# Moving the compressed branch's outputs into the local branch's PSUM banks in a hybrid attention layer

## The reference, cut to what matters

```
proj = rmsnorm(x) @ w_in
# attention: 8 heads of 128 in 2 key/value groups g, 4 heads r in each
s     = q @ kcmp * scale                         # compressed branch: 127 blocks
p_cmp = softmax(where(valid, s, NEG))
o_cmp = p_cmp @ vcmp
imp   = (p_cmp summed over the 4 heads) @ overlap # importance of 32 blocks
sel   = top 16 of imp (first and local blocks forced)
o_sel = softmax(q @ ks over selected blocks) @ vs # selected branch
o_win = softmax(q @ kw over 512 tokens) @ vw      # local branch
o     = g0 * o_cmp + g1 * o_sel + g2 * o_win
# pooling mixer: trailing means over 2/4/8/16 tokens minus the token, then a 256x256 matmul per group
h = x + concat(y_pool, o) @ w_out
h = h + (silu(n(h) @ w_gate) * (n(h) @ w_up)) @ w_down
h = h + (p @ w_ple_proj) * sigmoid(n(h) @ w_ple_gate);  out = rmsnorm(h)
```

## Time and profile before

| | |
|---|---|
| runs | 1813.19, 1814.67, 1815.13 us; median 1814.67 |
| profiled execution, its own time | 1814.66 us |
| its span on the slowest core (core 1) | 1813.1 us |
| spans of the 8 cores | 1808.7 to 1813.1 us |
| PE busy | 1678.0 us, 93% of the span |
| DVE, ACT, POOL busy | 578.7, 405.9, 279.6 us |
| attention stage, 320 to 616 us: PE busy | 241.90 of 296 us |

### The profile page before, as it was taken

The page is one execution under the profiler, slowest core; times in us unless marked ns, Lnnn a source line. Parts: engine busy times, 40 slices in busy tenths (PEclk is TensorE's granted clock), DMA queues, the critical chain, the costliest instruction groups (busy, mean ns, idle before and its releaser), DMA issues.

```text
span 1813.1 us, 25150 instructions; the slowest of 8 cores (1808.7 to 1813.1 us)
## 1 busy us (share of the span) xinstructions
PE 1678.0 (93%) x8998; PEld 825.4 (46%) x8998; DVE 578.7 (32%) x1386; ACT 405.9 (22%) x675; POOL 279.6 (15%) x339
## 2 busy tenths in 40 slices
PE   4799999788878999999999999999999999999994
PEld 1344544455545544444444444444444444444453
DVE  2663343554445313401122101311012200135556
ACT  3452212444436512100000000000000000133332
POOL 3232000012232133100000000000000000054321
PEclk9799999999989999999999999999999999999997
DMA  9565402011106920654039340583402934334413
GB/s 200 168 162 96 65 15 47 1 25 25 47 1 100 191 95 1 117 93 93 1 59 174 60 80 1 102 152 73 93 1 48 175 60 90 57 66 81 77 52 136
DMA packets 31323, 144.01 MB, mean 79 GB/s; under 512 B 4576, under 2 KB 9184, under 8 KB 22240
## 3 DMA queue, kind: packets, MB, share of 16 engines
q0 software_dynamic: 16416, 108.04, 34.0%
q1 hardware_dynamic: 14784, 34.35, 5.7%
HBM read 242.03 MB, written 8.39 MB: 138 GB/s over the span
## 4 chain that ended last, share of the span: by engine, by line
PE 84%; DVE 7%; DMA 3%; issue 3%; ACT 2%; DVEq 0%; POOL 0%; SPq 0%; ACTq 0%; POOLq 0%
PE ps L1215 17%; PE ps L1192 16%; PE ps L1189 16%; PE ps L511 11%; PE ps L1168 6%; PE ps L1293 5%; PE ps L869 3%; PE ps L738 2%; PE ps L754 2%; DMA arena<-c_sin 1%; DVE arena L1141 1%; DMA arena<-xin 1%; DVE arena L717 1%; PE ps L535 1%; DMA arena<-wup 1%
## 5 line engine op out<-in xcount | busy, mean ns | idle before, releaser
L1189 PE MATMUL ps<-arena 128*128 128x512 bf16 x1408 | 319.7, 379 | 2.0 <-DVE arena L1141 2.0
L1192 PE MATMUL ps<-arena 128*128 128x512 bf16 x1408 | 319.7, 380 | 0.8 <-DMA arena<-wup 0.8
L1215 PE MATMUL ps<-arena 128*128 128x512 bf16 x1408 | 304.9, 379 | 0.0
L1197 DVE TENSOR_TENSOR arena<-ps,arena 128x512 bf16<-128x512 f32 x88 | 60.9, 692 | 540.4 <-PE ps L1192 278.1
L1196 ACT ACTIVATE arena<-ps 128x512 f32<-128x512 f32 x88 | 52.6, 598 | 782.8 <-PE ps L1189 755.7
L1189 PEld LDWEIGHTS ps<-arena 128*128 128x128 bf16 x1408 | 137.8, 98 | 169.6 <-issue 4.9
L1192 PEld LDWEIGHTS ps<-arena 128*128 128x128 bf16 x1408 | 138.1, 98 | 168.1 <-issue 3.4
L1215 PEld LDWEIGHTS ps<-arena 128*128 128x128 bf16 x1408 | 137.8, 98 | 166.2 <-issue 0.6
L511 PE MATMUL ps<-arena 128*128 128x512 bf16 x896 | 208.2, 389 | 0.1
L1095 DVE TENSOR_TENSOR arena<-ps,arena 128x512 f32<-128x512 f32 x160 | 110.6, 691 | 275.2 <-PE ps L1215 202.4
L1107 POOL TENSOR_TENSOR arena<-arena 128x512 f32<-128x512 f32 (+2 forms) x98 | 115.4, 1178 | 232.0 <-ACT arena L1106 220.2
(11 more groups left out here) (146 smaller groups left out, 1145.1 us busy)
## 6 DMA issues: line engine op xcount, KB each, us to landing
arena<-wdown POOLq DMA_DIRECT2D x16, 1536.0 KB, 13.7
arena<-wgate POOLq DMA_DIRECT2D x22, 1024.0 KB, 9.5
arena<-wup POOLq DMA_DIRECT2D x22, 1024.0 KB, 11.0
arena<-xin SPq DMA_DIRECT2D x32, 512.0 KB, 5.5
arena<-wB POOLq DMA_DIRECT2D x20, 512.0 KB, 14.4
arena<-xT SPq DMA_DIRECT2D x16, 512.0 KB, 18.6
arena<-wout POOLq DMA_DIRECT2D x4, 2048.0 KB, 35.4
arena<-wpg POOLq DMA_DIRECT2D x4, 2048.0 KB, 23.4
```

The source lines that it names most:

```text
L1189: PE(lambda e, dc=dc: e.matmul(ps[pg][:], lhsT=wgu[sl][:, dc, half * 128:(half + 1) * 128], rhs=a2T[t][:, dc, :], start=(dc == 0), stop=(d ...
L1192: PE(lambda e, dc=dc: e.matmul(ps[pu][:], lhsT=wgu[sl + 1][:, dc, half * 128:(half + 1) * 128], rhs=a2T[t][:, dc, :], start=(dc == 0), sto ...
L1215: PE(lambda e, ci=ci: e.matmul(ps[pb][:], lhsT=wt_[:, ci, mm * 128:(mm + 1) * 128], rhs=hT[:, ci, t * 512:(t + 1) * 512], start=(ci == 0), ...
```

## The change

Three things change. (1) s1 writes the compressed outputs into banks 4 and 5, two heads in each, the banks of the local branch; only segment 0's, which is computed earlier, keeps banks 6 and 7. (2) s1 no longer closes a half-done unit, and the hold is gone: pieces come by credit alone. (3) s3 stands at step ntot-3 instead of ntot-5, ntot being the steps of the segment. The order of the heads in DVE's reads changes with the banks.

```diff
-    fstate = {"open": False, "hold": 0, "credit": 0.0}
+    fstate = {"open": False, "credit": 0.0}
...
         def bankof(r):
-            return (TB, 340) if r == 3 else (FB, 161 * r)
+            if sbank is not None:
+                return (TB, 340) if r == 3 else (FB, 161 * r)
+            return (4 + r // 2, 161 * (r % 2))
+        lead = (0, 3) if sbank is not None else (0, 2)
 
         def s1():
-            close_fill()
-            fstate["hold"] = 4
             for r in range(4):
                 bank, c0 = bankof(r)
...
-            r_, Br = branch_scale([(3, 4, ps[TB][:, 468:469]), (0, 3, ps[FB][:, 128:451:161])], [PB[TB], PB[FB]], 0, g, ot)
+            if sbank is not None:
+                den, Bden = [(3, 4, ps[TB][:, 468:469]), (0, 3, ps[FB][:, 128:451:161])], [PB[TB], PB[FB]]
+            else:
+                den, Bden = [(2, 4, ps[5][:, 128:290:161]), (0, 2, ps[4][:, 128:290:161])], [PB[5], PB[4]]
+            r_, Br = branch_scale(den, Bden, 0, g, ot)
...
-            if fstate["hold"] > 0:
-                fstate["hold"] -= 1
-            elif fill and fstate["credit"] >= 1.0 and len(fill) > 1:
+            if fill and fstate["credit"] >= 1.0 and len(fill) > 1:
                 pop_fill()
...
-                at.setdefault((0, min(4, ntot - 1), min(4, ntot - 1), 6, ntot - 5)[k], []).append(f)
+                at.setdefault((0, min(4, ntot - 1), min(4, ntot - 1), 6, ntot - 3)[k], []).append(f)
```

More of the change, by code:

```diff
@@ L786, in bankof @@
         def bankof(r):
-            return (TB, 340) if r == 3 else (FB, 161 * r)
+            if sbank is not None:
+                return (TB, 340) if r == 3 else (FB, 161 * r)
+            return (4 + r // 2, 161 * (r % 2))
+        lead = (0, 3) if sbank is not None else (0, 2)
         def s1():
-            close_fill()
-            fstate["hold"] = 4
             for r in range(4):
                 bank, c0 = bankof(r)
-                PE(lambda e, r=r, bank=bank, c0=c0: e.matmul(ps[bank][:, c0:c0 + 161], lhsT=pt[:, r, :], rhs=vcmp1[:, g, 0:161], start=(r in (0, 3)), stop=True, skip_group_check=True),
+                PE(lambda e, r=r, bank=bank, c0=c0: e.matmul(ps[bank][:, c0:c0 + 161], lhsT=pt[:, r, :], rhs=vcmp1[:, g, 0:161], start=(r in lead), stop=True, skip_group_check=True),
                    [Bpt, B_vcmp[g]], [PB[bank]])
-            r_, Br = branch_scale([(3, 4, ps[TB][:, 468:469]), (0, 3, ps[FB][:, 128:451:161])], [PB[TB], PB[FB]], 0, g, ot)
+            if sbank is not None:
[3 more added lines that the diff above has]
+            r_, Br = branch_scale(den, Bden, 0, g, ot)
             hold["r"] = (r_, Br)
@@ L799, in s1 @@
                 ib, Bi = impb[ii], B_imp[ii]
-                for n, r in enumerate((3, 0, 1, 2)):
+                for n, r in enumerate((2, 3, 0, 1)):
                     bank, c0 = bankof(r)
@@ L810, in s1b @@
             oa, B_oa = oaccs[oi % 3], B_oaccs[oi % 3]
-            for r in (3, 0, 1, 2):
+            for r in (2, 3, 0, 1):
                 bank, c0 = bankof(r)
```

## The result

The changed kernel takes 1794.7 us (median of 12 runs) against 1814.7 of the kernel before (12 runs, beside them): 20.0 us less, at a ratio of 0.9881 (95% interval 0.9841 to 0.9921). That is faster by 1.1%, and 9 us faster than the forecast of 1803.8; the range ended at 1795.

The account below looks back on a forecast made before the run. The prediction took about 54 us of idle PE in 320 to 616 us, nearly all ended by DVE's queue order, as the bound. Terms 11.7 - 7.9 - 3.9 - 6.4 - 2.4 - 2.0 = -10.9 gave 1803.8 us, range 1795 to 1813.

Parts of the forecast that it names:

- the clock: PE's granted clock in the attention stage: change put at zero, with 4 us to either side.
- term 6: Scores (L738) in steps paced by ACT, which the hold put in rows of four: idle time -2.0 us.
- term 1: s1's new wait for DVE's read of the local branch in banks 4 and 5: +11.7 us, bounds +6 and +17.
- term 2: PE's wait before the selection's transposes (L824), nearly all of it to go: -7.9 us.
- term 3: Output transposes (L724), whose bank 7 is no longer read by L813: wait gone, -3.9 us.
- term 4: Pieces (L869, L913) waiting for DVE, as compressed reads no longer hold bank 6: 12.1 to 5.7, -6.4 us.
- term 5: Pieces waiting for ACT's L917, as they now come every second step: 3.2 to 0.8, -2.4 us.
- A: Rival: without the hold, L877 queues behind compressed reads and DVE's backlog cancels the gain; +0.8, 1815.5 us; chance 0.22.
- B: Rival: new or longer waits in segments 8 to 14 bring clock dips of their own; +7, 1822 us; chance 0.07.
- C: Rival: full gain, segments 8 and 9 absorb waits, no piece waits for DVE, steps unpaced; -22, 1793 us; chance 0.12.
- D: Rival: gain doesn't reach the end, the output projection waiting for its weights or x; 1814 us; chance 0.03.

Follow-up runs that it names:

- e3: The kernel before without the hold, nothing else changed: 1843.2 us, ratio 1.0157 to the kernel before.
- e5: The changed kernel with the hold and the closing of a unit put back: 1798.7 us, ratio 0.9875 to the kernel before.
- e11: The kernel before with 16 unread matmuls in front of the selection's transposes of segments 3 and 11: 1812.5 us, ratio 0.9982.
- e8: The changed kernel with 16 and 10 unread matmuls in front of s1 in segments 8 and 9: 1793.4 us.
- e2: The kernel before with s3 two steps later and nothing else: 1804.8 us, ratio 0.994.
- e1: The kernel before with the new banks alone; hold, closing of a unit and s3's step stay: 1811.0 us, ratio 0.9992.
- e6: The changed kernel with s1 and s2 one step later in segments with ot of 2 or more: 1794.0 us.
- e7: The changed kernel with s1 and s2 two steps later in segments with ot of 2 or more: 1793.4 us.

## Why the prediction was right and wrong, by its own steps

The direction held, and so did nearly every wait; the gain was almost twice the forecast. Two steps failed: the clock was put at zero, and the hold's cost (term 6) was sized at 2.0 and looked for in listed waits. Means over the 8 cores, us:

| step | before | changed | measured | forecast |
|---|---|---|---|---|
| term 1, s1 | 18.5 | 28.4 | +9.8 | +11.7 |
| term 2, selection's transposes | 8.5 | 1.2 | -7.3 | -7.9 |
| term 3, output transposes | 3.9 | 0 | -3.9 | -3.9 |
| term 4, pieces behind DVE | 11.9 | 5.1 | -6.8 | -6.4 |
| term 5, pieces behind ACT | 3.2 | 0.9 | -2.3 | -2.4 |
| term 6, scores by ACT | 4.0 | 4.1 | +0.1 | -2.0 |
| small groups | 2.6 | 1.0 | -1.6 | 0 |
| idle in all | 52.6 | 40.7 | -11.9 | -10.9 |
| clock, PE busy | 13.2 | 10.1 | -3.1 | 0 |
| rest (waits not listed) | 230.5 | 225.8 | -4.7 | 0 |

**Term 1** was right in place, and within 2 us in size. The new waits stand where they were put; they come in pairs, as the two banks come free one after the other (segments 13 and 8, PE timeline of the changed kernel):

```profile
546.68 0.30 PE L795 MATMUL ps<-arena 128*128 128x161 bf16 x2 [1.49 <-DVE arena L717]
547.59 0.30 PE L795 MATMUL ps<-arena 128*128 128x161 bf16 x2 [0.61 <-DVE arena L717]
```

```profile
472.01 0.30 PE L795 MATMUL ps<-arena 128*128 128x161 bf16 x2 [4.10 <-DVE arena L717]
472.93 0.43 PE L795 MATMUL ps<-arena 128*128 128x161 bf16 x2 [0.61 <-DVE arena L717]
473.15 0.63 PE L738 MATMUL ps<-arena 128*128 128x512 bf16 x1
```

In segment 13 that is 1.49 + 0.61 = 2.1 us (forecast 2.4), in segment 8 4.10 + 0.61 = 4.7 (3.7), and in segment 9 2.5 (2.9).

**Terms 2 to 5** were right to 0.6 us each, by walking through the new order of PE and DVE with durations from the trace. (On core 1, from which the prediction read them, term 2 is -7.8.)

**Term 6** is one of the two steps that failed: a real effect, under-sized and looked for in the wrong place. The -2.0 was to come out of L738's listed waits, and these stayed (4.0, now 4.1). The hold's cost stands in waits that are not listed: with the hold the rest is 4.6 us higher in one pair of kernels (before and e3) and 5.7 in the other (e5 and changed), and from before to changed it falls by 4.7.

**The clock** is the other: "I put it at zero, with 4 us to either side". It gave 3.1 us while PE was busy; that is inside the 4, but the zero had no ground. The prediction reasoned from one wait, 3.23 us at 530.45 with matmuls at full speed behind it, that single waits don't lower the clock, and so set the removed waits against the new ones as equal. But the waits it removed were harmful ones: behind the 3.74 us of the earlier trace rows the granted clock was 0.73 in the next 10 us and the scores took 0.61 instead of 0.38. This could be read ahead of the run, in the same timeline, one record further on. e11 shows that dip to be a result of the wait and e8 shows it for the changed kernel's, and by e2 the s3 move alone gives back 4.4 us of clock. What was given back came from three places: the two long waits, and the deepest stretch of all, 490 to 500 us, which the prediction named and gave no term. It is at 1.00 in the changed kernel. e2 leaves it (0.58 on its page's core) and e1 shortens it (0.83), so the banks have a part in that; how, no run separates. The wait at 530.45 was a poor witness three times over: in e11 the same wait *is* followed by slow scores, 1.5 us later; in the kernel before the other 3.74 us come right behind it, with half-speed matmuls behind them; and in the very trace of the kernel before, on cores 0 and 3, this same wait of 3.23 us is followed by slow scores 1.6 us later. Its timeline and slice:

```profile
536.83 0.27 PE L824 MATMUL ps<-arena 128*32 128x128 bf16 x1 [3.74 <-DVE arena L821]
537.03 0.61 PE L738 MATMUL ps<-arena 128*128 128x512 bf16 x1
```

Its slices there:

```profile
530.00:540.00 10.00, 5.58 (x38) 3.43 (x38) 4.62 (x21) 2.77 (x5) 2.73 (x4) 0.79 0.00 0
```

The same place on core 0 of the kernel before:

```profile
526.98 0.44 PE L794 MATMUL ps<-arena 128*128 128x161 bf16 x4 [3.23 <-DVE arena L877]
...
528.53 0.58 PE L738 MATMUL ps<-arena 128*128 128x512 bf16 x1 [0.22 <-ACT arena L748]
...
529.34 0.63 PE L738 MATMUL ps<-arena 128*128 128x512 bf16 x1
...
533.36 0.27 PE L824 MATMUL ps<-arena 128*32 128x128 bf16 x1 [2.96 <-DVE arena L821]
```

There PE came to L824 later for being slow, so it waited 2.96 us instead of 3.74 and the transpose ran no later for it: part of what the low clock costs is taken back by a shorter wait.

The rule of the Trainium skill that the prediction weighed ("TensorE: Matmul & The Clock Gate", section "HAM oscillation — how this bites in real kernels": waits between bursts throttle the array, so that the next burst starts cold) agrees with e11 and e8 at the filled places: filling the waits and nothing else took the dips away there. Counting waits, as the prediction did with it (thirteen instead of nine), gave the wrong sign. Each of the two long waits cost some 1.7 us of clock beside its length (3.4 us of clock between the kernel before and e11). The new waits are not free either: in segments 13 and 14 of the changed kernel, where no pieces stand between the steps, scores of 0.63 follow s1's 2.1 us:

```profile
548.81 0.63 PE L738 MATMUL ps<-arena 128*128 128x512 bf16 x1
```

while 1.96 + 0.61 us in segment 12 (531.71) is followed by scores of 0.38 only. Length alone doesn't decide. Nor does the work around the wait alone: cores 0 and 1 of the kernel before do the same work around the same 3.23 us, and only core 0 is slow behind it. What decides, no run here separates.

**The rivals.** A (DVE's backlog takes it back) did not come: pieces behind DVE fell to 5.1 us (5.7 foreseen). It is what e6 and e7 ran into, however, and on the old banks it is +27.9 us (e3). B (a slower clock) fell: 0.96 in the stage, not under 0.93; but its places were right: the new dips stand in segments 8, 9, 13 and 14, four instead of six and of some 1.7 us each (0.83 in a slice) instead of 3, while the dips behind the waits that were removed went. C named nearly the right total, 1793, mostly by luck: term 1 came at +9.8 and not +6, term 4 at -6.8 and not -9; only its third condition, steps that run unpaced (-4.8), was met in size, by term 6's rest of 4.7. D did not come: PE is busy 79.63 of the 80 us behind the stage. That the stage's own bounds reached lower than 1795 (the clock's -4 on top of -17 is -21) was a fault of the range. Of the 8.8 us that the stage lost beyond the forecast, the clock and term 6 make 5.7; term 1 (1.9 less than forecast) and the small groups (1.6) make most of the rest.

## What to carry to other kernels

When a wait of PE is removed, read the records behind it as well: if the next matmuls take 0.6 us where the same ones take 0.38 elsewhere, the wait can be worth its length and that loss. Read it on several cores, since the same wait was followed by slow matmuls on some and not on others. Give an accumulation that is read late a bank that no other work in the loop needs; on a shared bank dropping the hold cost 28 us, on separate ones it gained 3. And where one engine's burst of reads releases everything, moving one consumer later helps only in places where nothing else queues behind the burst.

## What was not expected of the hardware

- PE's speed behind a wait depends on what it did in the wait: 16 matmuls with an unread result in 3.6 us ahead of the same release brought the next score from 0.61 to 0.38 us and the granted clock of the next slice from 0.73 to 1.00 (e11, the cores of the two pages). Work of no use made the stage 3.9 us shorter.
- Behind one and the same wait of 3.23 us, with the same work around it, cores 0 and 3 of the kernel before ran slowly 1.6 us later and core 1 did not. A single core's record behind a wait is no evidence that the wait is harmless.
- The clock's part of the gain was 3.1 of 19.7 us, with the mean granted clock of the stage moving only from 0.95 to 0.96. Length times (1 - granted clock) says 6.2, because before some 3 us of it fell into waits of PE, where low clock costs nothing.
- Four matmuls into two banks are released bank by bank: those of bank 5 started 0.91 us behind those of bank 4 (546.68 and 547.59), after a wait of 0.61. Two of the four DVE reads that take 1.72 us are 0.86.
